# Second layer's local attention: the matmul order goes from one query block per step to two blocks per round

## What is computed

```python
def block_attn(args):
    qn, kn, vn, mn = args
    logits = jnp.einsum('bqhgd,bkhd->bhgqk', qn, kn) * scale + bias
    logits = jnp.where(mn, logits, -jnp.inf)
    m = jnp.maximum(jnp.max(logits, axis=-1, keepdims=True), sink)
    e = jnp.exp(logits - m)
    w = e / (jnp.sum(e, axis=-1, keepdims=True) + jnp.exp(sink - m))
    return jnp.einsum('bhgqk,bkhd->bqhgd', w, vn)
```

## Time and profile before

| | us |
|---|---|
| median of 3 runs | 3024.66 (3024.32 to 3025.17) |
| the profiled execution's own time | 3023.84 |
| its span, first to last instruction | 3022.0 |
| TensorE busy | 2996.1 (99%) |
| VectorE busy | 1858.5 (61%) |
| ScalarE busy | 1148.5 (38%) |
| the stretch of the 32 steps' scores, 779.3 to 880.7 | 101.4 |

### The profile page before, as it was taken

One profiled execution on the slowest core, in us unless ns is written; L12 is line 12 of the kernel. 1 busy time (PEld: TensorE's weight loads), 2 busy tenths in 40 slices (PEclk: granted clock), 3 DMA queues, 4 the chain that ended last, 5 costly groups with the idle time before them and its releaser, 6 DMA issues.

```text
span 3022.0 us, 42980 instructions
## 1 busy us (share of the span) xinstructions
PE 2996.1 (99%) x15291; PEld 2533.6 (84%) x15291; DVE 1858.5 (61%) x3422; ACT 1148.5 (38%) x2083; POOL 1923.5 (64%) x1812
## 2 busy tenths in 40 slices
PE   8999999999999999999999999999999999999999
PEld 7877888888668888888777888999999998888887
DVE  7674544316865442160575236888868859878785
ACT  3466322102553221020454213444367754333333
POOL 7423766677337666776433576798965676766763
PEclk9999999999999999999999999999999999999999
DMA  7111222222212222222112223799989999999995
GB/s 241 70 43 42 91 98 98 98 98 105 77 43 105 98 98 98 98 93 97 69 68 68 83 97 113 239 329 327 335 297 329 335 363 383 380 363 362 360 366 194
DMA packets 175168, 547.68 MB, mean 181 GB/s; under 512 B 13667, under 2 KB 67076, under 8 KB 155140
## 3 DMA queue, kind: packets, MB, share of 16 engines
q1 hardware_dynamic: 117348, 338.81, 32.5%
q0 software_dynamic: 39168, 142.62, 12.4%
q10 hardware_dynamic: 18464, 63.70, 5.7%
HBM read 487.55 MB, written 57.40 MB: 180 GB/s over the span
## 4 chain that ended last, share of the span: by engine, by line
PE 95%; ACT 2%; DVE 2%; issue 1%; DMA 0%; ACTq 0%; DVEq 0%
PE banks L194 85%; PE banks L2998 2%; PE banks L2250 1%; PE banks L1151 1%; PE banks L2286 1%; PE banks L2265 1%; PE banks L1807 1%; PE banks L1845 1%; PE banks L1220 0%; PE banks L1823 0%; PE banks L2299 0%; PE banks L1210 0%; PE banks L1241 0%; PE banks L2918 0%; PE banks L1767 0%
## 5 line engine op out<-in xcount | busy, mean ns | idle before, releaser
L194 PE MATMUL banks<-memory,weights_split 128*128 128x512 f32 (+1 forms) x9456 | 2042.1, 373 | 9.1 <-DVE memory L578 8.5
L194 PEld LDWEIGHTS banks<-memory,weights_split 128*128 128x128 f32 x9456 | 1692.4, 188 | 279.4 <-issue 34.0
L3741 POOL TENSOR_SCALAR weights_split<-weights_raw 128x512 fp32r<-128x512 f32 x576 | 376.0, 662 | 739.7 <-issue 368.5
L3746 POOL TENSOR_TENSOR weights_split<-weights_raw,weights_split 128x512 fp32r<-128x512 f32 x576 | 767.6, 1344 | 0.2
L3576 POOL TENSOR_TENSOR weights_split<-weights_raw,weights_split 128x512 fp32r<-128x512 f32 x384 | 507.4, 1346 | 265.7 <-ACT weights_split L3375 263.8
L194 PE MATMUL banks<-weights_split,memory 128*128 128x512 f32 (+1 forms) x2880 | 646.4, 386 | 0.0
L194 PEld LDWEIGHTS banks<-weights_split,memory 128*128 128x128 f32 x2880 | 533.7, 188 | 108.9 <-issue 1.0
L3375 ACT ACTIVATE weights_split<-weights_raw 128x1024 fp32r<-128x1024 f32 x256 | 268.7, 1051 | 41.3 <-DMA weights_raw<-in_weights 24.0
L3078 DVE CUSTOM_DVE_ANT_0 memory<-memory,banks 128x1024 f32<-128x1024 f32 x144 | 173.7, 1215 | 64.5 <-DMA memory<-in_peer_u,memory 61.9
L712 DVE TENSOR_TENSOR banks<-banks,memory 128x512 f32<-128x512 f32 x88 | 61.4, 699 | 231.8 <-PE banks L194 231.7
L3570 POOL DMA_INDIRECT memory<-in_peer_v,memory x128 | 160.4, 1253 | 41.1 <-issue 26.6
(11 more groups left out here) (312 smaller groups left out, 2666.1 us busy)
## 6 DMA issues: line engine op xcount, KB each, us to landing
weights_raw<-in_weights SPq DMA_DIRECT2D x143, 1024.0 KB
weights_raw<-in_weights SPq DMA_DIRECT2D x257, 512.0 KB
routing<-memory ACTq DMA_DIRECT2D x12, 2048.0 KB, 11.8
hidden<-memory ACTq DMA_DIRECT2D x62, 384.0 KB
memory<-hidden SPq DMA_DIRECT2D x31, 768.0 KB
memory<-routing SPq DMA_DIRECT2D x30, 768.0 KB
window_rows<-memory ACTq DMA_DIRECT2D x1, 3064.0 KB, 25.7
chunk_rows<-memory ACTq DMA_DIRECT2D x1, 2556.0 KB, 10.7
```

The lines of the kernel that those rows point to most:

```text
L194: last = k.nc.tensor.matmul(out, left[a], right[b], start=start and n == 0, stop=stop and n == 2, skip_group_check=True)
L3741: k.nc.gpsimd.tensor_scalar(cut(high, n * PIECE, PIECE), cut(raw, n * PIECE, PIECE), 1.0, 1.0, ALU.mult, ALU.mult).then_inc(k.high_made, 1)
L3746: k.nc.gpsimd.tensor_tensor(cut(low, n * PIECE, PIECE), cut(raw, n * PIECE, PIECE), cut(high, n * PIECE, PIECE).bitcast(F32), ALU.subtract ...
```

## The change

TensorE's order is written in rounds d of two steps. A round holds `apply(2d - 4)`, `apply(2d - 3)`, `score(2d)`, `score(2d + 1)`, two units, `turn_probs(2d - 2)`, `turn_probs(2d - 1)`, two units, and in even rounds `sum_squares(d // 2 + 1)`. The loops of VectorE and ScalarE keep their order. Both steps' scores of a head lie in one bank now, 255 keys and the sink for each (the first key of a band, always masked, is left out, and its probability is set to zero once); VectorE waits for the second of them, since TensorE writes the bank until then, and only the even step's scores wait for `biased`. There is a fourth buffer for probabilities, and a bank for transposes is used in the new order.

```diff
-    for t in range(LAST + 1):
-        if 2 <= t <= STEPS + 1:
-            turn_uses["probs", t - 2] = len(turn_free)
-            turn_free.append((copied, t - 1))
-        if t % 4 == 0 and 2 <= t // 4 + 1 < PAIRS:
-            turn_uses["sums", t // 4 + 1] = len(turn_free)
-            turn_free.append((rooted, t // 4))
+    for d in range(TURNS + 1):
+        if d:
+            for t in (2 * d - 2, 2 * d - 1):
+                turn_uses["probs", t] = len(turn_free)
+                turn_free.append((copied, t + 1))
+        if d % 2 == 0 and 2 <= d // 2 + 1 < PAIRS:
+            turn_uses["sums", d // 2 + 1] = len(turn_free)
+            turn_free.append((rooted, d // 2))
...
+    def scores_of(t, f, sink=0):
+        return cut(score_banks[f].memory, (t % 2 + 1) * 2 * P - 1 - reach(t), reach(t) + sink)
...
-                else:
+                    for at in (2 * P - 1, 4 * P - 1):
+                        mm(cut(score_banks[f].memory, at, 1), k.const("ident"), cut(k.const("strict"), 0, 1), start=True,
+                           stop=True, skip_group_check=True)
+                elif t % 2 == 0:
                     pe.wait_ge(biased, 2 * (t - 1) + f + 1)
...
-        counts = [2] * 28 + [1, 1, 1, 1, 6, 6, 4]
-        for t in range(STEPS + 3):
-            if t < STEPS:
-                score(t)
-            advance(counts[t] // 2)
-            if 2 <= t <= STEPS + 1:
-                turn_probs(t - 2)
-            advance(counts[t] - counts[t] // 2)
-            if t % 4 == 0 and ("sums", t // 4 + 1) in turn_uses:
-                sum_squares(t // 4 + 1)
-            if t >= 3:
-                apply(t - 3)
+        counts = [(2, 2)] * 14 + [(1, 1)] * 2 + [(8, 4), (4, 0)]
+        for d in range(TURNS + 2):
+            if d >= 2:
+                apply(2 * d - 4)
+                apply(2 * d - 3)
+            if d < TURNS:
+                score(2 * d)
+                score(2 * d + 1)
+            advance(counts[d][0])
+            if 1 <= d <= TURNS:
+                turn_probs(2 * d - 2)
+                turn_probs(2 * d - 1)
+            advance(counts[d][1])
+            if d % 2 == 0 and ("sums", d // 2 + 1) in turn_uses:
+                sum_squares(d // 2 + 1)
...
         def biased_scores(t, f):
             i = t // 4
-            dve.wait_ge(scored, 2 * t + f + 1)
-            if t >= 3:
-                dve.wait_ge(turned_up, turn_uses["probs", t - 3] + 1)
+            dve.wait_ge(scored, 2 * (t + (t % 2 == 0)) + f + 1)
+            if t >= 4:
+                dve.wait_ge(turned_up, turn_uses["probs", t - 4] + 1)
...
+        for memory in probs:
+            v.memset(memory.rearrange("p (f n) -> p f n", f=2)[:, :, 0:1], 0.0).then_inc(small_made, 1)
```

More of the change, by code:

```diff
@@ L1680, in window_layer @@
 def window_layer(k, common, normed, after_norm):
-    STEPS, LAST, PAIRS, BAND = 32, 35, SW_HEADS // 2, 2 * P + 1
+    STEPS, LAST, PAIRS, BAND, TURNS = 32, 35, SW_HEADS // 2, 2 * P + 1, 16
     with k.scope(at=X_AT):
@@ L1691, in window_layer @@
         turned = [k.take(512) for _ in range(3)]
+        last_probs = k.take(2 * BAND)
+        assert k.pointer <= B_AT
     with k.scope(at=0):
-        probs = [k.take(2 * BAND) for _ in range(3)]
+        probs = [k.take(2 * BAND) for _ in range(3)] + [last_probs]
     with k.scope(at=B_AT):
@@ L1746, in width, with reach @@
         return P if t % 4 == 0 else 2 * P
+    def reach(t):
+        return min(width(t), 2 * P - 1)
     def buffer(t, f):
-        return cut(probs[t % 3], f * BAND + 2 * P - width(t), width(t))
+        return cut(probs[t % 4], f * BAND + 2 * P - width(t), width(t))
     def with_sink(t, f):
-        return cut(probs[t % 3], f * BAND + 2 * P - width(t), width(t) + 1)
+        return cut(probs[t % 4], f * BAND + 2 * P - reach(t), reach(t) + 1)
+    def scores_of(t, f, sink=0):
+        return cut(score_banks[f].memory, (t % 2 + 1) * 2 * P - 1 - reach(t), reach(t) + sink)
     def pair(memory, t):
@@ L1801, in score @@
                     score_banks[f].await_free(pe)
-                    mm(cut(score_banks[f].memory, 2 * P, 1), k.const("ident"), cut(k.const("strict"), 0, 1), start=True,
-                       stop=True)
-                else:
+                    for at in (2 * P - 1, 4 * P - 1):
+                        mm(cut(score_banks[f].memory, at, 1), k.const("ident"), cut(k.const("strict"), 0, 1), start=True,
+                           stop=True, skip_group_check=True)
+                elif t % 2 == 0:
                     pe.wait_ge(biased, 2 * (t - 1) + f + 1)
                 rows = slice(64 * f, 64 * f + 64)
-                mm(cut(score_banks[f].memory, 2 * P - width(t), width(t)), normed_q[i % 2][rows, n * P:(n + 1) * P],
-                   cut(key_pairs[rows, :], i // 2 * 512 + (n + 1) * P - width(t), width(t)), start=True,
-                   stop=True).then_inc(scored, 1)
+                mm(scores_of(t, f), normed_q[i % 2][rows, n * P:(n + 1) * P],
+                   cut(key_pairs[rows, :], i // 2 * 512 + (n + 1) * P - reach(t), reach(t)), start=True, stop=True,
+                   skip_group_check=True).then_inc(scored, 1)
         def await_turn_bank(use):
@@ L1937, in biased_scores @@
             i = t // 4
-            dve.wait_ge(scored, 2 * t + f + 1)
-            if t >= 3:
-                dve.wait_ge(turned_up, turn_uses["probs", t - 3] + 1)
+            dve.wait_ge(scored, 2 * (t + (t % 2 == 0)) + f + 1)
+            if t >= 4:
+                dve.wait_ge(turned_up, turn_uses["probs", t - 4] + 1)
             if f == 0 and t % 4 == 0 and i < 3:
                 dve.wait_ge(table_in[i], 16 if i < 2 else 16 * (PAIRS - 2))
-            at = 2 * P - width(t)
-            v.tensor_tensor_reduce(out=with_sink(t, f), in0=cut(score_banks[f].memory, at, width(t) + 1),
-                                   in1=cut(table, (2 * i + f) * BAND + at, width(t) + 1), scale=1.0, scalar=3e38,
+            v.tensor_tensor_reduce(out=with_sink(t, f), in0=scores_of(t, f, 1),
+                                   in1=cut(table, (2 * i + f) * BAND + 2 * P - reach(t), reach(t) + 1), scale=1.0, scalar=3e38,
                                    op0=ALU.add, op1=ALU.min, accum_out=one(shift, t, f)).then_inc(biased, 1)
@@ L1950, in even_out @@
             v.reciprocal(pair(inverse, t), pair(total, t)).then_inc(small_made, 1)
-            dve.wait_ge(small_made, t + 2)
+            dve.wait_ge(small_made, t + 6)
             for f in range(2):
@@ L1991, in vector @@
         opening_queries(1)
-        dve.wait_ge(small_made, 1)
+        dve.wait_ge(small_made, 5)
         for t in range(LAST + 1):
```

## The result

The changed kernel takes 3063.3 us in the median of four runs (3060.4 to 3066.7), the one before 3024.5: a ratio of 1.013 (95% interval 1.0118 to 1.0142), 38.8 us more. The direction was forecast, and the two idle gaps; the size wasn't. 3063.3 lies 2.3 us above the range, and the rise is one and a half times the 24.8 us of the sum.

What follows compares the result with a forecast made beforehand. TensorE was taken to bound the kernel, busy 99% of the span. Terms of 19.6, 2.7 and 2.5 us made +24.8 on a median of 3024.66, giving 3049.5 us, range 3039 to 3061.

Steps and rivals of the forecast that it cites:

- the two idle gaps: In each four steps TensorE idles waiting for ScalarE's copies: 3.1 us behind the sums of squares, 2.2 in the odd round.
- the sum: Whole stage: 19.6 us between first and last sums of squares, 2.7 ahead, 2.5 behind, together +24.8 us.
- The length of a group at full clock: Four steps, from one sums of squares to the next, take 17.7 us where they took 13.2.
- The price of a turn: TensorE turning from whole array to column halves, row halves and back costs 0.56 us; all turns saved, 9.2 us.
- The layout at nothing: Reading and writing 256 columns from odd places adds nothing; a rival had up to +6 us, over 3 us at chance 0.08.
- the one on the clock: Rival: TensorE's clock falls in six of the longer gaps, +10 us, 3060 us in all; chance 0.08.
- the front: Rounds 0 to 2, ahead of the first sums of squares: +2.7 us, with TensorE waiting 1.3 us for step 1's probabilities.
- its memsets at nothing: Tiny VectorE memsets ahead of the first scores: between nothing and 4 x 0.1 us, taken as nothing.
- The tail: Behind the last sums of squares: +2.5 us, with 40 units behind the last value product instead of 36.

Runs made afterwards that it cites:

- the gaps filled: Changed kernel plus unread matmuls between the two value products of rounds 3 to 14, five in odd rounds, three in even: 3054.3 us.
- the best kernel: Changed kernel with the orders of TensorE, ScalarE and VectorE all set by rounds, both copies behind the even step's exponents: 3019.5 us, 0.9984 of the kernel before.
- the kernel with those gaps alone: Changed kernel, but ScalarE copies step 4i - 1 ahead of the root, leaving only the 1.9 us gap of each group: 3040.1 us.
- a dense stretch: Kernel before with only waits added in both feed-forward layers, ahead of every group of 16 units: 3130.0 us, 1.035.
- the three with copies moved: Changed kernel with ScalarE's copies one step earlier, for step 4i - 1, step 4i + 1, or both: 3040.1, 3047.7 and 3023.2 us.
- the kernel with both copies early: Changed kernel, but ScalarE makes both copies of a round behind the even step's exponents: 3023.2 us, 0.9997 of the kernel before.

## Why the prediction was wrong

The steps that held:

- The gaps. Forecast 3.1 and 2.2 us in each group, measured 3.07 and 1.91; the waits forecast at 32 us, measured 29.4 + 3.0. (The prediction says that three units stood between the sums and the second copy's value product before; the code has four, and that way it is 6.3 us, which the "some 6 us" fits.) The path (root, table, exponents, copy; then inversion, normalising, odd scores, copy) is the one in the chain, and removing it on ScalarE alone takes the time back to 3023.2.
- The length of a group at full clock. Forecast 17.7 us; 18.05 in the mean with the gaps filled.
- The price of a turn. The two blocks cost what was reckoned to 0.01 us. The 9.2 us for all turns together no run shows; the best kernel gained 4.9.
- The layout at nothing: 3024.4.

The step that failed is the one on the clock. I saw that the trace of before had no gap longer than 1.4 us and could say nothing about longer ones, and then still gave that rival 0.08, left the clock out of the sum, and counted in the rival only the six longer gaps, at less than 1.7 us each, on the ground that the odd round waits for VectorE anyway. The runs show: in the profiled execution the clock fell behind all twelve gaps, the short ones too, and each fall lies on the path. Behind the long gap it doubles value product and scores, which VectorE waits for (1.4 us, 3.05 against 1.65), and behind the short one it stretches the units and the transposes (1.2 us by the kernel with those gaps alone; two units take 2.77 us in the timeline where they take 1.66 at full clock). Together that is about what a group is longer than with the gaps filled, 20.55 - 18.05 = 2.5 us. Filling the gaps, with 10 of the 12 falls gone, brought the time from 3063.3 to 3054.3.

Between the first and the last sums the time grew by 102.75 - 68.87 = 33.9 us where the sum had 19.6: five groups at 2.5 for the clock are 12.5, and 1.8 is left for the groups themselves. The Trainium skill, page "TensorE: Matmul & The Clock Gate", section "Why this matters for your kernels", was right in warning of long idle gaps between bursts. The trace agrees for the gaps of 3.07 us, and falls came behind gaps of 1.78 to 2.08 us as well. I should have taken it as a rival of even chance at least, since no row spoke against it.

The other term that was mis-sized is the front: from the first scores to the first sums, forecast +2.7, measured +5.3 (19.0 us against 13.65). The transposes of step 1 waited 2.4 us, not 1.3, and the clock fell once behind that. The first scores themselves begin 0.4 us later (779.73, before 779.33), where the prediction put its memsets at nothing; in the kernel with the layout alone they begin at 779.61, and its time is level with before within the interval. The tail was forecast at +2.5 and is +3.3, and holds the fall of double length.

So the 42.9 us of the profiled execution are 0.4 + 5.3 + 33.9 + 3.3. Of the 18.1 that they lie over the forecast, 12.5 are the groups' falls, and what is left of the front's 2.6 when the longer wait is taken off, 1.5, fits one more. The median is 38.8, 14.0 over the forecast, and its executions have no trace; that they had fewer or shorter falls is what their higher mean clock says. That 3063.3 lies only 2.3 us above the range is in part luck: the range was stretched to 3061 for a clock rival of six falls, and twelve were seen.

## What to carry to other kernels

When one engine's order is rewritten in coarser rounds, follow for each value that it takes what stands ahead of it in the other engines' unchanged orders: here two copies on ScalarE stood behind a root, a table load and exponents that used to be covered by 6 us of TensorE's work, and moving those two copies alone was worth 40 us. An idle gap of about 2 us or more on TensorE should be priced at its length plus a possible fall of its clock, which cost 1.2 to 1.7 us here, 2.2 where it was a long one, and came behind about half of the gaps of 1.8 to 3.4 us outside the changed kernel. Take the whole range between no fall and one behind every gap. Turning TensorE between the whole array and its halves cost 0.56 us a time and can be saved in pairs, once no other engine has to hurry for it; 4.9 us is what came of it here.

## What the runs showed of the hardware that I had not expected

- TensorE's clock fell to the lower level behind gaps as short as 1.78 us, with or without half-array matmuls around, but not each time. In the changed kernel it was 12 of 12. When the other gap of the group was removed, it was 3 of 6 gaps of 1.91 us and 4 of 6 of 3.07 us. In a dense stretch it was 4 of 8 of 2.08 us, 6 of 8 of 3.40 us and none of 8 of 1.65 us. Behind gaps of less than 1.65 us it didn't happen.
- The gap doesn't settle it alone. The same gap of 2.4 us ahead of the first transposes was followed by a fall in the changed kernel and the filled one, and by none in the three with copies moved; of the gaps of 1.8 us for the late keys one of three was. Why it was all of them in the changed kernel isn't settled; it wasn't tried to shift the gaps against each other.
- The changed kernel, with the most falls in the attention, varies more than others: 3060.4 to 3066.7 us in four runs, against 3022.5 to 3024.3 in ten runs of the kernel with both copies early. Mean clock and time go together in the four (0.992 for the slowest, 0.994 for the fastest).
- Useless matmuls in a gap made the kernel 9 us faster.
